# A hybrid decoder layer on one NeuronCore: differential attention with split scores and one flat sequence of steps

## The reference

```python
h = rmsnorm(x, norm_mix)
proj = h @ w_in                       # holds dq, dk, dv beside the other branches
q_d = dq.reshape(b, s, 4, 2, 64); k_d = dk.reshape(b, s, 4, 2, 64); v_d = dv.reshape(b, s, 4, 128)
s = einsum('bqhcd,bkhcd->bhcqk', q_d, k_d) * 64**-0.5 + bias[:, :, None]   # c: the two halves
s = where(causal, s, -1e30)
p = softmax(s, axis=-1)
a = p[:, :, 0] - lam * p[:, :, 1]
y_diff = einsum('bhqk,bkhe->bqhe', a, v_d)
```

## Time and profile before

| | us |
|---|---|
| median of 3 runs | 2996.05 (2992.53 to 2996.17) |
| the profiled execution | 3004.51 |
| its span | 3003.0 |
| differential attention, first to last matmul | 469.2 to 759.5 |
| the merge's first matmul | 761.1 |

### The profile page before, as it was taken

How to read it: one execution, slowest core, us unless ns; L and a number is a source line. 1 busy time by engine, 2 the same in 40 slices (tenths; PEclk the granted TensorE clock), 3 DMA queues, 4 the chain that set the end, 5 groups by cost and what they waited for, 6 DMA issues and landing times.

```text
span 3003.0 us, 47092 instructions
## 1 busy us (share of the span) xinstructions
PE 2808.7 (94%) x16548; PEld 2275.4 (76%) x16549; DVE 1480.1 (49%) x2566; ACT 1033.4 (34%) x1610; POOL 293.7 (10%) x308
## 2 busy tenths in 40 slices
PE   6988888888899999799999999999999999999995
PEld 3346664544566645489999999999899999999995
DVE  4334443444411114666666666666345554444554
ACT  2013332222311012145555555554233333333333
POOL 0000000000000012301111111111111111111111
PEclk9988888889999999599999999999999999999997
DMA  4000001000211153566676766666899999999995
GB/s 129 0 10 5 4 0 29 14 14 0 63 42 42 42 180 50 184 202 195 205 222 210 220 198 218 201 216 217 265 338 344 338 339 342 341 341 343 346 337 179
DMA packets 425339, 522.88 MB, mean 174 GB/s; under 512 B 29428, under 2 KB 336280, under 8 KB 425256
## 3 DMA queue, kind: packets, MB, share of 16 engines
q1 hardware_dynamic: 402504, 464.05, 47.6%
q0 software_dynamic: 18432, 57.20, 7.8%
q10 hardware_dynamic: 4352, 0.98, 0.2%
HBM read 482.23 MB, written 39.95 MB: 174 GB/s over the span
## 4 chain that ended last, share of the span: by engine, by line
PE 56%; issue 0%; DMA 0%; DVE 0%; ACT 0%; SPq 0%; POOLq 0%; POOL 0%; ACTq 0%
PE banks L1814 20%; PE banks L1824 19%; PE banks L1865 16%; PE banks L1806 1%; DVE arena L2108 0%; DMA arena<-acc_rows 0%; DMA acc_rows<-arena,rows 0%; ACT parts L1909 0%; DVE parts L2029 0%; SPq L1746 0%; ACT arena L2001 0%; ACT parts L1936 0%; ACT arena L1980 0%; DVE stat L2106 0%; POOLq L1772 0%
## 5 line engine op out<-in xcount | busy, mean ns | idle before, releaser
L1814 PEld LDWEIGHTS banks<-arena 128*128 128x128 f32 x5376 | 604.9, 192 | 8.2 <-issue 6.6
L1814 PE MATMUL banks<-arena 128*128 128x128 f32 x5376 | 605.2, 275 | 6.2 <-issue 6.2
L1824 PE MATMUL banks<-parts 128*128 128x256 f32 x4608 | 558.0, 284 | 7.1 <-issue 4.0
L1824 PEld LDWEIGHTS banks<-parts 128*128 128x128 f32 x4608 | 557.3, 193 | 8.7 <-issue 4.4
L1865 PE MATMUL banks<-parts 128*128 128x512 f32 x2160 | 498.3, 391 | 0.0
L1865 PEld LDWEIGHTS banks<-parts 128*128 128x128 f32 x2160 | 403.0, 188 | 82.1
L2025 DVE TENSOR_TENSOR parts<-arena,parts 128x1024 fp32r<-128x1024 f32 x264 | 315.3, 1222 | 128.3 <-ACT parts L1929 127.8
L2048 DVE TENSOR_SCALAR arena<-banks,arena 128x128 f32<-128x128 f32 (+1 forms) x528 | 181.4, 393 | 335.4 <-PE banks L1814 335.4
L2029 DVE TENSOR_TENSOR parts<-arena,parts 128x1024 fp32r<-128x1024 f32 x192 | 233.8, 1223 | 197.0 <-ACT parts L1936 195.7
L1929 ACT ACTIVATE parts<-arena 128x1024 fp32r<-128x1024 f32 x264 | 269.7, 1054 | 88.4 <-PE banks L1865 44.9
L1936 ACT ACTIVATE parts<-arena 128x1024 fp32r<-128x1024 f32 x192 | 201.1, 1053 | 178.0 <-PE banks L1824 117.7
(11 more groups left out here) (287 smaller groups left out, 2674.4 us busy)
## 6 DMA issues: line engine op xcount, KB each, us to landing
arena<-in_w SPq DMA_DIRECT2D x264, 1024.0 KB, 7.6
arena<-in_w SPq DMA_DIRECT2D x66, 2048.0 KB, 12.7
arena<-in_w_in SPq DMA_DIRECT2D x27, 512.0 KB, 5.0
arena<-in_x SPq DMA_DIRECT2D x16, 512.0 KB, 4.4
h_rows<-arena POOLq DMA_DIRECT2D x10, 512.0 KB, 7.5
acc_rows<-arena SPq DMA_DIRECT2D x8, 512.0 KB, 4.3
arena<-acc_rows SPq DMA_DIRECT2D x8, 512.0 KB, 7.7
out<-arena SPq DMA_DIRECT2D x8, 512.0 KB, 5.7
```

The lines of the kernel that those rows point to most:

```text
L1814: last = nc.tensor.matmul(bank(g, 2 * (c % 2) + s)[:, a * JOB:a * JOB + P], w1[c][:, s, k, a * P:(a + 1) * P], xt[:, k, 0:P], start=(k == ...
L1824: last = nc.tensor.matmul(bank(g, 2 * (c % 2) + s)[:, a * JOB:(a + 1) * JOB], first_part[p][:, y, k, :], x[:, k, :], start=(k == 0 and y = ...
```

## The change

Differential attention alone is changed, in four ways.

1. Scores in two parts. q and k are written as a high part (the value written as type fp32r) and a low part (the value less the high part). For each half c, tile `q_c[c]` holds the high part of q in its 64 partitions and the low part in the other 64; `k_c[h % 2][c]` holds the high part of k twice. One fp32r matmul with 128 rows of contraction gives (q high + q low) times k high; a second with 64 rows adds q high times k low. The tiles lie in `parts`, 32 KiB for each partition, which take the place of an arena segment that is no longer needed.
2. A unit of projection is 512 tokens of q or of k of one head (8 matmuls); there are 16. Units 0 and 1 (first halves of k and q of head 0) stand ahead of everything; the other 112 matmuls are dealt out over steps 0 to 26, four a step (eight in step 0), two behind the scores of the first half and two behind those of the second. All of them use bank 7; unit n+1 may begin only when the low part of unit n is made (`lo_made`). `apply` has bank 6 alone, so it waits for the `store_y` of the step before.
3. When a unit is complete (units 2 to 15: in step 0, 2, 4, ... 26), ACT makes the high part behind its `copy_early` (`high`: four copies of 64 partitions for a k, two for a q), and DVE makes the low part behind its `combine` and ahead of its `store_y` (`low`: two operations).
4. The loop over heads is gone: 32 steps in one sequence, u = 8 x head + i, so score(u+1) of the next head follows in step 7 of this one. Head 0's weights are loaded in the MLA stage, those of heads 1 and 2 at the start of this stage.

```diff
+            sp.wait_ge(q_rotated, MLA_HEADS + 1)
+            load_head(g, io, sp, 0)
...
+DIFF_STEPS = TT * DIFF_HEADS
+KEY, QUERY = 0, 1
...
+def unit_of(n, general):
+    kinds = ((KEY, 0), (KEY, 1), (QUERY, 0), (QUERY, 1)) if general else ((KEY, 0), (QUERY, 0), (KEY, 1), (QUERY, 1))
+    return (n // 4,) + kinds[n % 4]
+def units_before(u, general):
+    return 4 * (u // TT) + (4 if u % TT >= 4 else 3 if general else 2)
+def unit_plan(general):
+    ahead = 4 if general else 2
+    fill = [[] for u in range(DIFF_STEPS)]
+    if general:
+        for u in range(24):
+            fill[u] = [(4 + u // 2, 4 * (u % 2) + k) for k in range(4)]
+    else:
+        for u, ks in enumerate((range(0, 8), range(8, 12), range(12, 16))):
+            fill[u] = [(2 + k // KT, k % KT) for k in ks]
+        for u in range(3, 27):
+            fill[u] = [(4 + (u - 3) // 2, 4 * ((u - 3) % 2) + k) for k in range(4)]
+    done = [[n for n, k in fill[u] if k == KT - 1] for u in range(DIFF_STEPS)]
+    return ahead, fill, done
...
+    part = [g.parts[0][:, n * SEQ:(n + 1) * SEQ] for n in range(8)]
+    q_c, k_c, k_low = part[0:2], [part[2:4], part[4:6]], part[6:8]
+    first, second = slice(0, DIFF_DIM), slice(DIFF_DIM, P)
...
+    unit_bank = lambda n, general: bank(g, 6 if n % 2 and n < unit_plan(general)[0] else 7)
...
+            for h in (1, 2):
+                load_head(g, io, sp, h)
+            sp.wait_ge(projected, 4)
+            load_head(g, io, sp, 3)
...
-                    for s, w in ((0, w_q), (1, w_k)):
-                        pe.wait_ge(w, 16 * h + 16)
-                        for c in range(2):
-                            for k in range(KT):
-                                last = nc.tensor.matmul(bank(g, 2 * s + c), wst[:, s, k, :], ht[:, k, c * HALF:(c + 1) * HALF],
-                                                        start=(k == 0), stop=(k == KT - 1))
+                ahead, fill, done = unit_plan(general)
+                def project(n, k):
...
-                            rows = slice(c * DIFF_DIM, (c + 1) * DIFF_DIM)
-                            for a in range(0, keys, HALF):
-                                n = min(HALF, keys - a)
-                                last = nc.tensor.matmul(bank(g, 2 * c + a // HALF)[:, 0:n], q_t[rows, i * P:(i + 1) * P],
-                                                        k_t[rows, a:a + n], start=True, stop=True)
-                            last.then_inc(scored, 1)
...
+                def project(n, k):
+                    h, kind, c = unit_of(n, general)
+                    if k == 0:
+                        pe.wait_ge(g.w_head[h % 3], 64 if h == 3 else 32)
+                        if n >= ahead:
+                            pe.wait_ge(lo_made, n)
+                        elif n >= 2:
+                            pe.wait_ge(lo_made, n - 1)
+                    last = nc.tensor.matmul(unit_bank(n, general), head_weights(g, h)[:, kind, k, :], ht[:, k, c * HALF:(c + 1) * HALF],
+                                            start=(k == 0), stop=(k == KT - 1))
+                    if k == KT - 1:
                         last.then_inc(projected, 1)
-                    pe.wait_ge(q_copied, h + 1)
-                    pe.wait_ge(k_copied, h + 1)
-
-                    def score(i):
-                        keys = (end(i) + 1) * P
-                        for c in range(2):
-                            s = 2 * i + c
-                            if s >= 2:
-                                pe.wait_ge(exped, base + s - 1)
-                            rows = slice(c * DIFF_DIM, (c + 1) * DIFF_DIM)
-                            for a in range(0, keys, HALF):
-                                n = min(HALF, keys - a)
-                                last = nc.tensor.matmul(bank(g, 2 * c + a // HALF)[:, 0:n], q_t[rows, i * P:(i + 1) * P],
-                                                        k_t[rows, a:a + n], start=True, stop=True)
-                            last.then_inc(scored, 1)
-
-                    def turn(i):
-                        pe.wait_ge(combined, ub + i + 1)
-                        for grp in range(1 + end(i) // 4):
-                            if grp == 0 and i >= 1:
-                                pe.wait_ge(pt_act, ub + i)
-                            if grp == 1 and late_before(i):
-                                pe.wait_ge(pt_dve, late_before(TT) * h + late_before(i))
-                            for kt in range(4 * grp, min(4 * grp + 4, end(i) + 1)):
-                                last = nc.tensor.transpose(bank(g, 4 + grp)[:, (kt % 4) * P:(kt % 4 + 1) * P],
-                                                           prob[:, 2 * (i % 2), kt * P:(kt + 1) * P], g.ident[:, :])
-                            last.then_inc((turned0, turned1)[grp], 1)
-
-                    def apply(i):
-                        pe.wait_ge(pt_act, ub + i + 1)
-                        if end(i) >= 4:
-                            pe.wait_ge(pt_dve, late_before(TT) * h + (late_before(i) + 1))
-                        pe.wait_ge(y_out, ub + i + 1)
-                        for kt in range(end(i) + 1):
-                            last = nc.tensor.matmul(bank(g, 6 + i % 2)[:, 0:DIFF_V], prob_t[:, i % 2, kt * P:(kt + 1) * P],
-                                                    v[:, kt, bass.ds(h * DIFF_V, DIFF_V)], start=(kt == 0), stop=(kt == end(i)))
-                        last.then_inc(applied, 1)
-
-                    score(0)
-                    for i in range(TT):
-                        if i + 1 < TT:
-                            score(i + 1)
-                        if i == TT - 1:
-                            apply(i - 1)
-                        turn(i)
-                        if 1 <= i < TT - 1:
-                            apply(i - 1)
-                    apply(TT - 1)
+                def score(u, c):
+                    h, i = divmod(u, TT)
+                    keys, s = (end(i) + 1) * P, 2 * u + c
+                    if c == 0:
+                        pe.wait_ge(lo_made, units_before(u, general))
+                    if s >= 2:
+                        pe.wait_ge(exped, s - 1)
+                    rows, cols = (first, second)[c], slice(i * P, (i + 1) * P)
+                    for a in range(0, keys, HALF):
+                        n = min(HALF, keys - a)
+                        out = bank(g, 2 * c + a // HALF)[:, 0:n]
+                        nc.tensor.matmul(out, q_c[c][:, cols], k_c[h % 2][c][:, a:a + n], start=True, stop=False)
+                        last = nc.tensor.matmul(out, q_c[c][rows, cols], k_low[h % 2][rows, a:a + n], start=False, stop=True)
+                    last.then_inc(scored, 1)
...
+                def apply(u):
+                    h, i = divmod(u, TT)
+                    pe.wait_ge(pt_act, u + 1)
+                    if end(i) >= 4:
+                        pe.wait_ge(pt_dve, late_before(u) + 1)
+                    pe.wait_ge(y_out, u + 2)
+                    for kt in range(end(i) + 1):
+                        last = nc.tensor.matmul(bank(g, 6)[:, 0:DIFF_V], prob_t[:, u % 2, kt * P:(kt + 1) * P],
+                                                v[:, kt, h * DIFF_V:(h + 1) * DIFF_V], start=(kt == 0), stop=(kt == end(i)))
+                    last.then_inc(applied, 1)
...
+                for n in range(ahead):
+                    for k in range(KT):
+                        project(n, k)
+                score(0, 0)
+                score(0, 1)
+                for u in range(DIFF_STEPS):
+                    half = len(fill[u]) // 2
+                    if u + 1 < DIFF_STEPS:
+                        score(u + 1, 0)
+                    for n, k in fill[u][:half]:
+                        project(n, k)
+                    if u + 1 < DIFF_STEPS:
+                        score(u + 1, 1)
+                    for n, k in fill[u][half:]:
+                        project(n, k)
+                    if u == DIFF_STEPS - 1:
+                        apply(u - 1)
+                    turn(u)
+                    if 1 <= u < DIFF_STEPS - 1:
+                        apply(u - 1)
+                apply(DIFF_STEPS - 1)
 
             either(g, pe, attend)
...
+                def low(n):
+                    h, kind, c = unit_of(n, general)
+                    cols, src = slice(c * HALF, (c + 1) * HALF), unit_bank(n, general)
+                    dve.wait_ge(hi_made, n + 1)
+                    if kind == KEY:
+                        k0, k1 = k_c[h % 2]
+                        nc.vector.tensor_tensor(k_low[h % 2][first, cols], src[first], k0[first, cols], ALU.subtract)
+                        nc.vector.tensor_tensor(k_low[h % 2][second, cols], src[second], k1[second, cols], ALU.subtract).then_inc(lo_made, 1)
+                    else:
+                        nc.vector.scalar_tensor_tensor(out=q_c[0][second, cols], in0=src[first], scalar=DIFF_SCALE, in1=q_c[0][first, cols],
```

(69 more changed lines are left out.)

155 lines of the change are left out of this document (60 added, 95 removed).

## The result

The changed kernel takes 3015.3 us (7 runs, 3006.0 to 3017.2), the kernel before 2996.2 in the same comparison: ratio 1.0057, 95% interval 1.0044 to 1.007. Forecast were 2969 and a range of 2948 to 2990. In a second comparison (e_again) the ratio is 1.0033, interval 1.0016 to 1.0049.

The account below looks back on a forecast made before the run. In differential attention (290.4 us), TensorE projects alone, then shares an unfilled chain with DVE and ACT. The stage sums to 249.3 us, 41 less; minus 14 for the clock, 27 less: median 2996.05 to 2969, range 2948 to 2990.

Parts of the forecast that it names:

- an fp32r matmul of 512 columns costs 0.235 us: Price of the new score matmuls on TensorE, taken from an existing fp32r row; float32 score records cost 0.431 us.
- the other end, 0.431: Upper end of the price of fp32r score matmuls, meaning no saving at all; it would cost 29 us.
- rival 2: Copies and products on ACT and DVE take 1.2 us more at each of 14 waits: 17 us, 2986; chance 0.15.
- rival 3: Slower: sparse stretches and new waits hold TensorE's clock down; at a clock of 0.80, 3004; chance 0.08.
- The clock term: In the differential stage, waits lower TensorE's clock: 14 us lost, ends 0 and 32; forecast with it has chance 0.55.
- 58.9: Microseconds summed for eight steps of the changed stage at full clock, where a head took 71.4 before.
- the first matmul follows the branch: At the stage's start, PE's branch over the general path takes 5.2 us and the first matmul comes right after it.
- the bubble behind them: After units 0 and 1, two ACT copies, two DVE products and hand-over before the first score: 2.6 us.
- 14 waits on DVE's low parts: TensorE idles before projections until DVE's low part is done, 14 times 1.9 to 2.7 us, 30 us in all.
- earns nothing: Early load of head 0's weights was held to be hidden by PE's branch of 5.2 us at the stage's start.
- Rival 1: The clock holds and the waits are a little shorter than summed: gain 41 + 3 us, 2952; chance 0.22.
- The reading that score halves on different partitions don't overlap: In the kernel before, eight score records of 64 rows take 3.45 us, 0.431 each, so they were read as sequential.

Follow-up runs that it names:

- e_again: The changed kernel run once more without edits, for a second profile and more times; ratio 1.0033 to the kernel before, differential stage 302 us.
- e_rows128: Changed kernel with the low score product taking all 128 rows instead of 64, adding low times low; 2982.6 us, ratio 0.9953 to the kernel before.
- e_warm2: e_rows128 plus four unused float32 matmuls of 256 columns at the head of steps that wait for a finished unit; 2968.2 us, ratio 0.9885 to the kernel before.
- e_warm: e_rows128 plus unused float32 matmuls, placed in the step that finishes a unit, not the one that waits; 3000.3 us, ratio 1.0002 to the kernel before.
- e_f32flat: Changed kernel's flat schedule with float32 64-row scores, one copy per unit and no low parts; 2968.6 us, ratio 0.9911 to the kernel before.

## Why the prediction was wrong

**The step that failed** is "an fp32r matmul of 512 columns costs 0.235 us ... I take 0.235, the row of the same type and size". The row was of matmuls that all use 128 rows; the new ones alternate between 128 and 64, and 192 times in the stage a weight load of 0.19 us is open: 0.43 us from start to start at 512 columns, 36 us of TensorE's time in all. Taking the open loads away (e_rows128) gave 28.5 us back. The prediction named the other end, 0.431, with a price of 29 us (its own sum is 144 x 0.196 = 28), and set it aside; no rival had it, as rival 2 was copies and rival 3 the clock. That 29 and 28.5 agree is luck: 29 was priced by the column, but the load costs the same for 128 columns as for 512, so it comes to 36, of which 8 went into longer waits.

**The clock term** was right in kind: 14 forecast. e_rows128 has the forecast price of scores and takes 273 us; with the waits filled (e_warm2) it is 257, so 16 us are shown, not all by the waits alone, as e_warm says. Nearly all of it (15 us) lies in the first three rounds, 1.4 in the tail. What is left, 257 - 249.3 = 8 us, isn't in the later rounds (59.2 for 58.9) but in the start (34.1 for 31.9), the first round (60.9) and the tail (31.5 for 28.4), where the clock is 0.89, 0.97 and 0.95; I didn't take it apart further. So of the 38.2 us between 301.5 and 263.3 the open loads are 28.5, the clock 16 - 14 = 2, and 8 are this rest. The changed kernel's own tail (36.3 us at 0.72 for 28.4) has open loads in it too: 3.4 of its 8 us go with them.

**Right:** the first matmul follows the branch with 7.16 us of issue; units 0 and 1 take 16.1 us (16.0) and the bubble behind them 2.7 (2.6); 14 waits on DVE's low parts of about 2 us, though only seven of them stand before a projection and the seven on the low part of a q before the scores; DVE isn't the bound; copies and products within 0.4 us a unit; the experts don't move; no blocks of 27.6 us between heads. The early load "earns nothing" held against before, but undoing it alone costs 1.2 us, since three heads are now loaded at once. **Rival 1** fell with the clock. **Rival 2** had the right place, but only some 0.3 to 0.4 us a unit. **Rival 3** forecast 3004 at a clock of 0.80; the outcome lies near, by another cause: 0.90 in the stage, hardly other than the 0.89 of before. The reading that score halves on different partitions don't overlap was wrong (e_f32flat).

Why the median moved by 19 us and the stage by 11 stays partly open. The MLA stage varies by up to 14 us between executions; the share of runs with the lower clock may have differed between the two sets (not shown), and the second comparison (e_again, +9.8 us in the medians) fits the stage better.

## What to carry to other kernels

Take the price of a matmul from a row in which the matmuls before and after it use the same number of rows as they will in your kernel, not only the same type and columns. Where matmuls of 64 and of 128 rows would alternate, use all 128 rows if the extra term is harmless; grouping them by rows gained only 4 us here. A new wait of 2 us on TensorE can cost more than 2 us: put the producer's chain behind other work of TensorE, and if a hole stays, see whether useless matmuls in it keep the clock up. When a change combines a schedule and an arithmetic trick, price and test them apart: here one gained 30 us and the other lost 41.

## What was not expected of the hardware

- A weight load of 0.19 us is hidden behind a matmul on the same rows (loads 0.23 us apart) and open when the rows change between 128 and 64 of them (0.43 apart), both ways. Float32 halves on rows 0 to 63 and 64 to 127 run side by side: eight records in 1.36 us (e_f32flat).
- Filling 14 waits with 56 useless matmuls made the stage 16 us shorter; 52 of them one step too early made it 17 us longer (e_warm).
- 52 more MATMUL records (26 matmuls) in one stage went with 137 us of issue in another, 12.4 at a time, and 131 instruction packets on one queue; with 104 or 112 more, on the same or the sister kernel, there was none of it.
- Unchanged MLA code takes 256 to 270 us from one execution to the next, at a clock of 0.89 to 0.84.
